# Down projections of a two-layer transformer: six of 22 chunk pairs as seven block products

## The reference

```python
def conv_ffn(h, w_gate, w_up, conv_w, conv_b, w_down):
    a = causal_dwconv(h @ w_gate, conv_w, conv_b)
    return (jax.nn.silu(a) * (h @ w_up)) @ w_down      # (256 x 5632) @ (5632 x 2048)
...
    h = rmsnorm(x, g[2])
    x = x + rmsnorm(conv_ffn(h, ...), g[3])            # once a layer
```

## Time and profile before

| | us |
|---|---|
| median of 3 runs | 2114.49 |
| lowest, highest run | 2114.43, 2115.53 |
| span of the profiled execution | 2113.3 |
| TensorE busy in it | 2104.6 |
| VectorE, ScalarE busy in it | 1336.3, 1064.2 |

### The profile page before, as it was taken

The page is one execution under the profiler, slowest core; times in us unless marked ns, Lnnn a source line. Parts: engine busy times, 40 slices in busy tenths (PEclk is TensorE's granted clock), DMA queues, the critical chain, the costliest instruction groups (busy, mean ns, idle before and its releaser), DMA issues.

```text
span 2113.3 us, 34635 instructions
## 1 busy us (share of the span) xinstructions
PE 2104.6 (100%) x12177; PEld 1803.3 (85%) x12177; DVE 1336.3 (63%) x2048; ACT 1064.2 (50%) x1627; POOL 286.4 (14%) x461
## 2 busy tenths in 40 slices
PE   9999999999999999999999999999999999999999
PEld 9987888888888888888999977888888888888887
DVE  7665676766766754445876654576766767754444
ACT  6675554444444444434666776554444444444443
POOL 4452000000000000000065773000000000000000
PEclk9999999999999999999999999999999999999999
DMA  7444455555565565554773334455565565565554
GB/s 256 151 159 154 166 194 194 181 191 187 172 204 181 187 213 187 188 188 155 235 251 121 101 111 135 155 200 189 179 193 184 180 199 186 182 215 190 188 187 133
DMA packets 111008, 381.42 MB, mean 180 GB/s; under 512 B 14194, under 2 KB 18754, under 8 KB 110402
## 3 DMA queue, kind: packets, MB, share of 16 engines
q1 hardware_dynamic: 108466, 373.63, 53.6%
q10 hardware_dynamic: 2448, 6.53, 0.9%
HBM read 377.97 MB, written 2.14 MB: 180 GB/s over the span
## 4 chain that ended last, share of the span: by engine, by line
PE 97%; DVE 1%; ACT 1%; DMA 0%; issue 0%; ACTq 0%; DVEq 0%
PE set L764 32%; PE set L842 30%; PE set L768 16%; PE set L1058 10%; PE set L1132 2%; PE set L900 1%; PE set L1106 1%; PE set L1154 1%; PE set L932 1%; PE set L1108 1%; PE set L1156 0%; PE set L974 0%; DVE wlo L1851 0%; PE set L1222 0%; PE set L1223 0%; DMA raw<-in_stream 0%
## 5 line engine op out<-in xcount | busy, mean ns | idle before, releaser
L1851 DVE TENSOR_TENSOR wlo<-raw,whi 128x1024 fp32r<-128x1024 f32 x703 | 859.9, 1233 | 560.1 <-ACT whi L1389 558.3
L1389 ACT ACTIVATE whi<-raw 128x1024 fp32r<-128x1024 f32 x703 | 736.9, 1056 | 725.8 <-PE set L768 351.2
L764 PE MATMUL set<-hs,whi 128*128 128x512 f32 x2896 | 952.7, 395 | 0.6 <-ACT whi L1487 0.3
L768 PE MATMUL set<-hs,wlo 128*128 128x256 f32 x2896 | 681.9, 281 | 0.0
L768 PEld LDWEIGHTS set<-hs,wlo 128*128 128x128 f32 x2896 | 534.8, 188 | 60.0 <-DVE wlo L1851 0.2
L764 PEld LDWEIGHTS set<-hs,whi 128*128 128x128 f32 x2896 | 497.2, 189 | 69.8 <-issue 0.8
L842 PE MATMUL set<-whi,hid 128*128 128x512 f32 x1360 | 374.6, 395 | 0.0
L842 PEld LDWEIGHTS set<-whi,hid 128*128 128x128 f32 x1360 | 255.1, 188 | 63.6 <-DVE wlo L1851 0.6
L842 PE MATMUL set<-wlo,hid 128*128 128x512 f32 x680 | 215.8, 395 | 0.0
L1058 PE MATMUL set<-hs,whi 128*128 128x256 f32 x1280 | 213.3, 286 | 0.3 <-DVE wlo L1851 0.3
L1058 PEld LDWEIGHTS set<-hs,whi 128*128 128x128 f32 x1280 | 176.6, 189 | 3.0 <-DVE wlo L1851 1.1
(11 more groups left out here) (219 smaller groups left out, 1449.0 us busy)
## 6 DMA issues: line engine op xcount, KB each, us to landing
raw<-in_stream SPq DMA_DIRECT2D x703, 512.0 KB, 3.4
gain_rows<-rows ACTq DMA_DIRECT2D x4, 1024.0 KB, 5.9
xT<-in_x SPq DMA_DIRECT2D x8, 256.0 KB, 7.7
out_y<-out_f SPq DMA_DIRECT2D x8, 256.0 KB, 2.4
bo_rows<-rows ACTq DMA_DIRECT2D x1, 768.0 KB, 9.1
wg_raw<-in_w_gates ACTq DMA_DIRECT2D x1, 768.0 KB, 4.6
raw<-in_stream SPq DMA_DIRECT2D x2, 256.0 KB, 4.3
bo_last<-rows ACTq DMA_DIRECT2D x1, 256.0 KB, 11.7
```

The source lines that it names most:

```text
L764: return mm(sets[set_of(u)][:, t, 0:2 * w], whi[:, slot, cols], r, start=first, stop=final)
L768: return mm(sets[set_of(u)][:, t, w:2 * w], wlo[:, slot, cols], r[:, 0:w], start=False, stop=False)
L1389: A(whi[:, slot, :], raw[:, slot, :], ACT.Copy).then_inc(hi_ready, 1)
L1851: V.tensor_tensor(wlo[:, slot, :], raw[:, slot, :], whi[:, slot, :].bitcast(F32), ALU.subtract).then_inc(lo_ready, 1)
```

## The change

Two neighbouring units (k = 0 and 1, then k = 2 and 3) are now worked together, since a block product needs both halves of the columns. For six of the 22 chunk pairs (`FOLDED` = chunks 4, 7, 10, 13, 16, 19) the 2x2 by 2x2 block product (two token tiles, two contraction tiles, two column halves) is computed with seven block products in place of eight, by Winograd's form of Strassen's scheme. Each block product is still three matmuls. The work around them is new: VectorE adds the parts of `hid` together (`hid_sum`), makes four sums of them (`fold_h`) and four sums of weight blocks (`fold_w`), ScalarE rounds those sums and VectorE subtracts for their low parts. Three of the seven products go into the output's banks directly; four go to banks of `sets[1]`, where they add up over the six folds (the shares). At the end of a pair of units VectorE adds the shares into `y` (`sum_shares`), and they are added where the banks are emptied (`bias_y`); for the last unit of a layer two share sums are split in two parts and TensorE adds them into the banks with a product by the identity (`add_shares`). The chunk order of a pair is 8 plain chunks (6 in the second pair of a layer), a fold (two chunks), 4 plain chunks, a fold, and so on; the second pair ends with two chunks of k = 2 and four of k = 3. SP fetches the chunks in that order. The `gain_rows` transfer and the norms behind the layers stay.

```diff
+FOLDED = (4, 7, 10, 13, 16, 19)
+FOLDS = len(FOLDED)
+PLAIN = [c for c in range(CHF) if c not in FOLDED]
+def down_order(lead):
+    order = [(k, c) for k in range(CK) for c in PLAIN[:lead[k]]]
+    for q, c in enumerate(FOLDED):
+        order += [(0, c), (1, c)]
+        if q < FOLDS - 1:
+            order += [(k, PLAIN[lead[k] + 2 * q + m]) for m in range(2) for k in range(CK)]
+    return order + [(k, c) for k in range(CK) for c in PLAIN[lead[k] + 2 * (FOLDS - 1):]]
+DOWN_ORDERS = down_order((5, 3)), down_order((4, 2))
...
+def summed_apart(u):
+    return is_down(u) and u not in (DN0 + 3, DN1 + 3)
...
+            def fetch_down(u):
+                for i, (k, c) in enumerate(down_chunks(u)):
+                    g = first_chunk(u) + i
+                    before = fold_of(u, i - RING)
+                    if before is None:
+                        sp.wait_ge(lo_ready, g - RING + 1)
+                    else:
+                        sp.wait_ge(fold_w_made, 3 * (folds_before(u) + before + 1))
+                        sp.wait_ge(lo_ready, first_chunk(u) + fold_at(u, before) + CK)
+                    sp.dma_start(raw[:, g % RING, :], stream[first_chunk(u + k) + c]).then_inc(raw_in[g % RING], 16)
...
+            def folded_down(u, n, g):
+                q = folds_before(u) + n
+                kt = CK * FOLDED[n]
+                first, final = n == 0, n == FOLDS - 1
+                def product(bank, h_hi, h_lo, w_hi, w_lo, start, stop):
+                    mm(bank, h_hi, w_hi, start=start, stop=False)
+                    mm(bank, h_hi, w_lo, start=False, stop=False)
+                    return mm(bank, h_lo, w_hi, start=False, stop=stop)
+                def share(b, i, w_hi, w_lo):
+                    return product(sets[1][:, b, :], fold_h_hi[:, i], fold_h_lo[:, i], w_hi, w_lo, first, final)
+                def tile(j, t):
+                    return hid[:, kt + j, t * P:(t + 1) * P], hid[:, kt + j, S + t * P:S + (t + 1) * P]
+                a, b = g % RING, (g + 1) % RING
+                upper, lower = slice(0, UNIT), slice(UNIT, CW)
+                if first:
+                    pe.wait_ge(evacuated, UT * u)
+                    if u in (DN0 + 2, DN1 + 2):
+                        pe.wait_ge(shares_summed, 5 * (q // FOLDS))
+                pe.wait_ge(lo_ready, g + CK)
+                pe.wait_ge(fold_h_low, q + 1)
+                product(sets[0][:, 2, :], fold_h_hi[:, 3], fold_h_lo[:, 3], whi[:, b, lower], wlo[:, b, lower],
+                        False, False).then_inc(fold_used, 1)
+                pe.wait_ge(fold_w_low, 2 * q + 1)
+                share(3, 2, fold_w_hi[:, 1], fold_w_lo[:, 1]).then_inc(fold_used, 1)
+                share(2, 0, fold_w_hi[:, 0], fold_w_lo[:, 0]).then_inc(fold_used, 1)
+                pe.wait_ge(fold_w_low, 2 * q + 2)
+                share(1, 1, fold_w_hi[:, 2], fold_w_lo[:, 2]).then_inc(fold_used, 1)
+                product(sets[0][:, 1, :], *tile(1, 1), fold_w_hi[:, 3], fold_w_lo[:, 3], False, False).then_inc(fold_used, 1)
+                product(sets[1][:, 0, :], *tile(0, 0), whi[:, a, upper], wlo[:, a, upper], first, final)
+                product(sets[0][:, 0, :], *tile(1, 0), whi[:, a, lower], wlo[:, a, lower], False, False).then_inc(chunk_used, CK)
+            def add_shares(layer):
+                pe.wait_ge(filled, 6)
+                pe.wait_ge(share_low, TT * (layer + 1))
+                for t in range(TT):
+                    for part in (fold_w_hi, fold_w_lo):
+                        mm(sets[0][:, CK + t, :], ident_r[:], part[:, t], start=False, stop=False)
...
@@ on ScalarE @@
+            def fold_split(u, n):
+                q = folds_before(u) + n
+                g = first_chunk(u) + fold_at(u, n)
+                a, b = g % RING, (g + 1) % RING
+                act.wait_ge(fold_h_made, q + 1)
+                A(fold_h_hi[:], fold_h[:], ACT.Copy).then_inc(fold_h_high, 1)
+                if n > 0:
+                    split(g - CK)
+                    split(g - 1)
+                act.wait_ge(fold_w_made, 3 * q + 1)
+                A(fold_w_hi[:, 0:2], fold_w[:, 0:2], ACT.Copy).then_inc(fold_w_high, 1)
+                act.wait_ge(raw_in[a], 16 * (g // RING + 1))
+                act.wait_ge(raw_in[b], 16 * ((g + 1) // RING + 1))
+                act.wait_ge(chunk_used, g - RING + CK)
+                A(whi[:, b, UNIT:CW], raw[:, b, UNIT:CW], ACT.Copy)
+                A(whi[:, a, :], raw[:, a, :], ACT.Copy).then_inc(hi_ready, CK)
+                act.wait_ge(fold_w_made, 3 * q + 3)
+                A(fold_w_hi[:, 2:4], fold_w[:, 2:4], ACT.Copy).then_inc(fold_w_high, 1)
+                split(g + CK)
+                split(g + CK + 1)
...
@@ on VectorE @@
+            def fold_split(u, n):
+                q = folds_before(u) + n
+                g = first_chunk(u) + fold_at(u, n)
+                a, b = g % RING, (g + 1) % RING
+                kt = CK * FOLDED[n]
+                h11, h21 = hid_sum[:, 0, 0:P], hid_sum[:, 0, P:S]
+                h12, h22 = hid_sum[:, 1, 0:P], hid_sum[:, 1, P:S]
+                w11, w21 = raw[:, a, 0:UNIT], raw[:, a, UNIT:CW]
+                quarters = raw[:, a:a + CK, :].rearrange("p s (j f) -> p (s j) f", j=CK)
+                if q > 0:
+                    dve.wait_ge(fold_h_made, q)
+                V.tensor_tensor(hid_sum[:], hid[:, kt:kt + CK, 0:S].bitcast(F32), hid[:, kt:kt + CK, S:2 * S].bitcast(F32),
+                                ALU.add).then_inc(fold_h_step, 1)
+                if q > 0:
+                    dve.wait_ge(fold_used, 5 * (q - 1) + 4)
+                dve.wait_ge(fold_h_step, 3 * q + 1)
+                V.tensor_tensor(fold_h[:, 0], h21, h22, ALU.add).then_inc(fold_h_step, 1)
+                V.tensor_tensor(fold_h[:, 2], h11, h21, ALU.subtract)
+                dve.wait_ge(fold_h_step, 3 * q + 2)
+                V.tensor_tensor(fold_h[:, 1], fold_h[:, 0], h11, ALU.subtract).then_inc(fold_h_step, 1)
+                dve.wait_ge(fold_h_step, 3 * q + 3)
+                V.tensor_tensor(fold_h[:, 3], h12, fold_h[:, 1], ALU.subtract).then_inc(fold_h_made, 1)
+                if n > 0:
+                    split(g - CK)
+                    split(g - 1)
+                dve.wait_ge(raw_in[a], 16 * (g // RING + 1))
+                dve.wait_ge(raw_in[b], 16 * ((g + 1) // RING + 1))
+                V.tensor_tensor(fold_w[:, 0:2], quarters[:, 2:4], quarters[:, 0:3:2], ALU.subtract).then_inc(fold_w_made, 1)
+                dve.wait_ge(fold_h_high, q + 1)
+                V.tensor_tensor(fold_h_lo[:], fold_h[:], fold_h_hi[:].bitcast(F32), ALU.subtract).then_inc(fold_h_low, 1)
+                if q > 0:
+                    dve.wait_ge(fold_used, 5 * q)
+                dve.wait_ge(fold_w_made, 3 * q + 1)
+                V.tensor_tensor(fold_w[:, 2], fold_w[:, 1], w11, ALU.add).then_inc(fold_w_made, 1)
+                dve.wait_ge(fold_w_made, 3 * q + 2)
+                V.tensor_tensor(fold_w[:, 3], w21, fold_w[:, 2], ALU.subtract).then_inc(fold_w_made, 1)
+                dve.wait_ge(fold_w_high, 2 * q + 1)
+                V.tensor_tensor(fold_w_lo[:, 0:2], fold_w[:, 0:2], fold_w_hi[:, 0:2].bitcast(F32), ALU.subtract).then_inc(fold_w_low, 1)
+                dve.wait_ge(hi_ready, g + CK)
+                V.tensor_tensor(wlo[:, b, UNIT:CW], raw[:, b, UNIT:CW], whi[:, b, UNIT:CW].bitcast(F32), ALU.subtract)
+                V.tensor_tensor(wlo[:, a, :], raw[:, a, :], whi[:, a, :].bitcast(F32), ALU.subtract).then_inc(lo_ready, CK)
+                dve.wait_ge(fold_w_high, 2 * q + 2)
+                V.tensor_tensor(fold_w_lo[:, 2:4], fold_w[:, 2:4], fold_w_hi[:, 2:4].bitcast(F32), ALU.subtract).then_inc(fold_w_low, 1)
+                split(g + CK)
+                split(g + CK + 1)
+            def sum_shares(u):
+                k = 0 if u in (DN0, DN1) else 2
+                done = 5 * (folds_before(u) // FOLDS)
+                def part(k, t):
+                    return y[:, CK * k:CK * (k + 1), t, :]
+                def share(b):
+                    return sets[1][:, b, :].rearrange("p (a f) -> p a f", a=CK)
+                dve.wait_ge(chunk_used, first_chunk(u) + fold_at(u, FOLDS - 1) + CK)
+                V.tensor_copy(part(k, 0), share(0)).then_inc(shares_summed, 1)
+                dve.wait_ge(shares_summed, done + 1)
+                V.tensor_tensor(part(k + 1, 0), share(1), part(k, 0), ALU.add).then_inc(shares_summed, 1)
+                dve.wait_ge(shares_summed, done + 2)
+                V.tensor_tensor(part(k, 1), share(3), part(k + 1, 0), ALU.add).then_inc(shares_summed, 1)
+                dve.wait_ge(shares_summed, done + 3)
+                V.tensor_tensor(part(k + 1, 1), share(2), part(k, 1), ALU.add).then_inc(shares_summed, 1)
+                V.tensor_tensor(part(k + 1, 0), share(2), part(k + 1, 0), ALU.add).then_inc(shares_summed, 1)
...
+            def down_pair(u, evacs, norm_next=False):
```

(23 more changed lines are left out.)

183 lines of the change are left out of this document (144 added, 39 removed).

## The result

| | before | after |
|---|---|---|
| median of the runs, us | 2114.9 (2114.43 to 2115.53, 4 runs) | 2103.39 (2102.85 to 2104.1, 4 runs) |
| span of the profiled execution, us | 2113.3 | 2101.7 |
| TensorE busy, us, and its matmuls | 2104.6, 12177 | 2089.8, 12113 |
| VectorE busy, us | 1336.3 | 1502.4 |

The ratio is 0.9946, with a 95% interval of 0.9932 to 0.996. The changed kernel is faster by 0.54%, 11.5 us; 2103.6 had been forecast.

What follows compares the result with a forecast made beforehand. TensorE, busy 2104.6 of 2113.3 us, was taken as the bound. 14.9 us of matmuls less 4.0 of stalls gave 10.9, span 2102.4, plus 1.2 for runs: 2103.6 us; own range 2101 to 2106 (0.60), overall 2099.5 to 2110.

Steps and rivals of the forecast that it cites:

- Removed and added matmuls: TensorE, down projections: 72 matmuls less in folds, 8 identity matmuls more, net 64 at 0.2333 us, 14.9 us gained.
- The inner folds cost nothing: At 20 folds VectorE's chain of 9.9 us ends 1.1 us ahead of TensorE, period 16.1 us: no stall.
- The turning point: Chain length to a fold's low parts at which the whole gain is lost: 11.5 us, 16% longer.
- Operation by operation on VectorE: VectorE's work for a fold priced singly: 128-column sums 0.28 us, 512 columns 0.68, splits 1.23; 13.3 us a period.
- Overlap of independent operations: On VectorE, an operation not reading the one before starts 0.09 us ahead of its end, as in four splits.
- The first rival: Joins cost double: VectorE's fold operations do not overlap, stalls 4.4 us a layer, 2108.5 us; chance 0.18.
- First fold of a layer: TensorE waits for low parts after chunk 9 lands late: stall 0 to 0.7 us, taken as 0.3 a layer.
- First fold of the second pair: VectorE needs 28.3 us against TensorE's 28.0: stall 0.3, or 0.75 with slower transfers, taken as 0.5 a layer.
- Identity products: Three chunks behind the last fold, TensorE waits for the shares' low parts: 1.2 us a layer, bounds 0.9 and 1.7.
- The norm behind the layer: VectorE's 2.94 us idle ahead of the reciprocal takes the third unit's emptying: no cost; if not, 1 us a layer.
- Sum: Gain 14.9 us less stalls of 4.0 over both layers: 10.9 us, span 2102.4, runs 2103.6.
- no stall at all: Rival: the bare 14.9 us are gained, with no waits at the joins, 2099.6 us; chance 0.07.

Runs made afterwards that it cites:

- The two runs with longer chains: Changed kernel with one unread VectorE operation (1024 columns) added per fold: 2110.23 us, ratio 0.9978; with a second of 512 columns: 2124.4 us, 1.0047.
- the repeat: The changed kernel run again, unchanged, as base for the other experiments: 2103.09 us, ratio 0.9944 to the kernel before.
- the last experiment: Changed kernel with identity products one held chunk later and ScalarE's square-root table load moved behind a layer's first four down splits: 2098.99 us, ratio 0.9926.

## Why the prediction was right, step by step

- *Removed and added matmuls* (14.9 us): right in number, 64 fewer, and nearly in price. A plain chunk goes at 0.2333 us a matmul, a fold at 0.232; over 24 folds that is 0.6 us more gain than the sum had. The new order alone differs by 0.2 us, with an interval around no change.
- *The inner folds cost nothing*: right. The period is 16.07 (16.1), the low parts end 1.17 us ahead where 1.1 and the way of 0.17 had been forecast. The two runs with longer chains put the slack at 1.0. The turning point was forecast for a chain of 11.5 us, 16% longer than 9.9; 1.735 us, 17.5%, made it 0.47% slower than before. By the forecast's working, 24 folds late by 1.735 - 1.1, this would have come 4.3 us above the kernel before, and it came 9.8 above: the first folds of the pairs lengthen by the whole 1.7, which that sum had left out, and the slack was 1.0.
- *Operation by operation on VectorE*: right. 128-column sums last 284 and 292 ns with 0.20 to the next start (0.28 and 0.20), 512 columns 0.68 to 0.69 (0.68), 1024 columns 1.22. Its busy time grew by 166 us; TensorE waited for it at the joins alone.
- *Overlap of independent operations* (0.09): right. In the changed kernel `fold_w` at 781.43 + 1.22 ends at 782.65, and `fold_h_lo`, which does not read it, starts at 782.57; between 783.17 + 0.68 = 783.85 and its reader at 783.89 there is none. So the rule of the Trainium skill that I had set against it ("VectorE: DVE Perf Modes", "The DRAIN you can't avoid") holds here for an operation that reads the one before, and in no row shown for the others. The same section also allows an exception that the prediction passed over, "A next op that is not held starts earlier"; the overlaps of 0.08 to 0.09 us in these rows agree with that. The first rival (2108.5), which hung on it, did not come.
- *First fold of a layer* (0.3): 0.6 and 0.5 in the two layers, 0.6 and 0.4 in the repeat; twice too small, but inside its bounds of 0 to 0.7. What decided was the landing of chunk 9, as forecast. The reason for its lateness was misread: I put it on the transfers alone, but behind them stood a table load of 1.28 us on ScalarE in front of the four splits. With the load moved and all else as in the run with the identity products later, the stall was gone. The earlier trace rows show the splits late behind ScalarE, and I took their start as given without asking what ScalarE did just before.
- *First fold of the second pair* (0.5): 0.1. This step was wrong, and beneath its lower bound of 0.3. The sum of 28.3 us was too long by 0.4 in one place, the emptying of the first pair's banks. These are the rows of VectorE that bound it:

```profile
865.92 1.28 DVE L2326 TENSOR_TENSOR y<-set,y 128x512 f32<-128x512 f32 x2
...
869.01 2.36 DVE L2071 TENSOR_TENSOR wlo<-raw,whi 128x1024 fp32r<-128x1024 f32 x2 [0.26 <-ACT whi L1563]
871.28 1.28 DVE L2326 TENSOR_TENSOR y<-set,y 128x512 f32<-128x512 f32 x2
...
874.37 3.50 DVE L2071 TENSOR_TENSOR wlo<-raw,whi 128x1024 fp32r<-128x1024 f32 x3 [0.26 <-ACT whi L1563]
...
884.31 1.22 DVE L2130 TENSOR_TENSOR wlo<-raw,whi 128x1024 fp32r<-128x1024 f32 x1
```

  Two sums into `y` and two gains, with all their waits for ScalarE, take 3.09 us each time (865.92 to 869.01, 871.28 to 874.37), 6.2 in all, where 2.4 + 4.2 = 6.6 had been counted with fuller waits for the squares and the rounding. The rest of the sum is met: from the last fold's end at 857.79 to the end of the low parts, 884.31 + 1.22 = 885.53, it is 27.74, with the way 27.9, and TensorE comes after 28.0. So it had 0.1 to spare and was just in time. The longer chain roughly agrees: with 1.135 us more the fold is 34.11 us behind the last of the first pair, 1.24 late, where 1.135 - 0.1 = 1.0 was to be expected.
- *Identity products* (1.2): 1.24 by the starts, and what their move gave back agrees.
- *The norm behind the layer* (0): right; 1.34 us of idle time left ahead of the reciprocal, where the forecast had about 1.
- *Sum*: the stalls are 3.8 us for both layers where 4.0 were forecast, but only because two errors cancel: the first folds of the layers cost 0.5 more than forecast, those of the second pairs 0.8 less. With the 0.6 that the folds' pace gave, the two stages are 11.8 us shorter where 10.9 were forecast. The profiled execution hid part of this, since it reached the first stage 0.94 later and won back 0.69 between the layers: forecast span 2102.4, measured 2101.7. The forecast of the runs has one more error, the 1.2 us added to the span. Every run of the kernel before and of the changed one whose own span is on record is 1.7 to 1.8 us longer than that span; the 1.2 came from setting the median of three runs beside the span of one execution that, by this offset, took some 2115.0 (an estimate). With 1.7 the forecast would have been 2104.1, 0.7 above the 2103.4 measured. That it was met to 0.2 us is luck; the terms are known to about 1 us.

The rival "no stall at all" (2099.6) was wrong for this kernel, but the two edits of the last experiment bring it about: 2099.0.

## What to carry to other kernels

Where one engine is full and work is moved to another, count the chain from the moment its inputs are free to the moment the full engine comes, operation by operation, in steps from start to start: the sum over a period fitted (15.0 of 16.07 us) where the chain was late by 0.74 us each time. Expect the cost at the joins, where the steady pattern begins and ends, and try first to move the consumer a few matmuls back, behind work that doesn't need the late data: six matmuls of other work ahead of it took 2.5 us of waiting away with no instruction changed. Ask of every start that is taken from a row what the engine ahead of it did just before; a table load of 1.28 us in front of four splits had cost a wait in two kernels.

## What the runs showed that I had not expected

- With the same bytes and the same share of the queues (0.56, against 0.57), a transfer of 512 KB takes 4.0 us in the median from issue to landing over the whole changed kernel, against 3.4 before. The pairs of transfers that go out at once behind a fold look like the cause, but most of it is there without them: in the run with the new order and no folds the median is 3.9. In the down projections of layer 0 and of layer 1 it is 3.3 and 3.3 us before, 3.8 and 4.2 with the new order alone, and 4.1 and 4.2 in the changed kernel. Between 20 and 740 us, where nothing was changed, it lies between 3.5 and 4.0 from run to run, so a few tenths mean little; what the rest comes from is open.
- The listed idle time of TensorE is less than the stall that the starts give: 1.00 against 1.24 at the identity products, 0.37 against 0.6 at the first fold. A wait of 0.1 us shows only in a first matmul of 0.47 to 0.50 in place of 0.39.
- The releaser "issue" at the first fold is not the engine's own delay. It vanished when VectorE's and the transfer's lateness did, in the last experiment.
- Delaying a transfer of 1 MB that nobody needed yet did not bring the urgent one in time; it only made a transfer for the next fold late.
